# A streaming encoder step on one core: x's tail loaded first, the first chunk's factors and evictions moved, and one addition moved at the end

## The chip, the cores and the metric

The kernel runs on one core of one Trainium2 chip. The metric is the time on the device in microseconds, smaller being better. Before the change it is the median of three runs, 586.95 us, with 585.12 and 587.8 as the ends.

## The reference

One inference step of a one-layer encoder over 512 prompt frames, 64 frames of a running stream ("sample") and 16 meta tokens, model width 1024, all in fp32:

```python
h = rmsnorm(x, norm1_g) @ w_in            # 1024 -> 2304: rq, rk, rv, rg, sq, sk, sv
rq, rk = rope(rq), rope(rk) * 64 ** -0.5  # retention: 4 heads, 64 wide, values 128
sq, sk = rope(rmsnorm(sq)), rope(rmsnorm(sk))       # 8 query and 2 key heads of 64
o_r = rmsnorm(retention(rq, rk, rv, state)) * silu(rg)
o_s = window_attention(sq, sk, sv, meta_k, meta_v, sinks)    # window 128, chunks of 64
x = x + concat(o_r, o_s) @ w_out
x = x + moe(rmsnorm(x, norm2_g))          # best of 4 groups, best 2 of its 8 experts, SwiGLU, 256 wide
```

It also returns the retention states and the newest 128 rows of keys and values, for the prompt and for the sample.

## The kernel before

**Tiles.** The tokens lie in five tiles: tiles 0 to 3 hold 128 prompt frames each, tile 4 ("the tail", `TAIL`) the 64 sample frames and the 16 meta tokens. They are worked in the order tail, 0, 1, 2, 3 (`ORDER`). The input projection is cut into five chunks of columns: first SKV (keys and values of the attention, 256 wide), then SQ (its queries), RQK, RV and RG, each 512 wide; two halves of the output projection follow. Each chunk and tile is one job on TensorE in two halves of the contraction (four blocks of 128 each).

**Precision.** x and the weights are split into a high part (rounded by a cast) and a low part (the difference). For a weight entry, ScalarE casts (L1522, `hi`) and GpSimd subtracts (L859, `lo`). For x, TensorE transposes four blocks against the identity (L986), DVE multiplies by norm1's factors into `part` (L1718), ScalarE casts to `xT_hi` (L1464), and DVE subtracts to `xT_lo` (L1705). Every product is three matmuls (L1038), or two with both parts of the 64 sample rows side by side in the columns of one weight load (L1032). For that second form DVE copies the sample's low parts beside the high ones (L1756), which `xT_end` does at its end.

**Rows' factors.** The squares of x are summed by ScalarE (`xsq`, L1457). `rstd1` on DVE makes the reciprocal roots for all five tiles in twelve small steps (L1725 and the helper at L286 to L296). Evictions of the first chunk (ScalarE, L1478 and L1479) multiply by them; `sums` squares the keys (ScalarE L1497, DVE reduces), `root` takes their roots on DVE, `post` rotates keys (from L1804) with tables that `tables` makes (L1743: norm factor times cosine and sine, for keys and for queries), and the tail's own keys before that.

**The order.** `plan()` writes one list of steps from `before[s]`, job `s`, `after[s]` and `behind[s]`, where s counts the half jobs: 0 to 9 are SKV's, 10 on are SQ's. Every engine goes through the same list and issues what is its own, so the order of steps in that list is the order of the instructions in each engine's queue. In the list, `hi`/`lo` are weight entries 0 to 3 (SKV) and 4 to 11 (SQ), `xT` the transposes of a tile's half with what follows them. The accumulators of SKV's tail and tile 0 are the two that SQ's first jobs use again, so that SQ starts when these two are evicted. SQ's tile 1 waits for the tail's q, which DVE sums from two parts (L1987). `cache_in` and `meta_v` are ScalarE's issues of small transfers (the cache of keys, values and state; shifted copies of the values), and `meta_v` also one copy on DVE (L1849).

**Loading.** Transfers are issued by three queues. SyncE's begins with norm1's factors `g1T`, the identity, the sample's x and the meta tokens, then weights and x of tiles 1 and 3, then SQ's weights; ScalarE's begins with weights and x of tiles 0 and 2; GpSimd's loads five small tensors (`small_in`).

**The experts.** 32 experts go through in 16 pairs. SyncE streams their weights through 18 buffers of 1 MB, which lie partly where the attention's tensors were, so that the first loads wait for the retention's last rows and later ones for the pairs to free a buffer. Rows are gathered, passed through, and scattered by GpSimd.

**The end.** Each tile's two rows of expert output are read back. DVE adds the two for tiles 0 and 4 (`row_in`, L2234), GpSimd for tiles 2 and 3 (L963), TensorE for tile 1. DVE then adds the last pairs' part from the accumulators (`sums_in`, L2283), in the order of the tiles, and SyncE writes each tile out:

```python
for i in (2, 3):
    dve.wait_ge(rows_clear, 2 + i)    # GpSimd's addition of tile i is done
    sums_in(i)
row_in(4)
sums_in(4)
```

Of the kernel before, what the change touches and what calls it, by code (L numbers as in the profile page):

```python
# [7 lines left out]
ALU = mybir.AluOpType  # L8
# [82 lines left out]
def plan():  # L91
# [17 lines left out]
    before[0] += weights(0, 1) + turned(0) + weights(2, 3) + turned(1) + [("small_in",)]  # L109
    before[1] += [("xsq", ORDER[0])] + turned(2)  # L110
    before[2] += weights(4)
    before[3] += [("xsq", ORDER[1])] + turned(3) + weights(5)
    before[4] += [("xsq", ORDER[2])] + weights(6, 7)
    before[5] += weights(8) + turned(4) + [("xsq", ORDER[3]), ("xsq", ORDER[4]), ("xT_end",), ("rstd1",)] + weights(9)
    before[6] += weights(10) + [("evict", SKV, t) for t in ORDER[:3]] + [("sums", SKV, t) for t in ORDER[:3]]
    before[6] += weights(11) + [("tables",)]
# [16 lines left out]
    after[s + 1] += [("post", SKV, TAIL), ("post", SKV, 0)]  # L133
    after[s + 2].append(("cache_in",))
    after[s + 3].append(("meta_v",))
# [164 lines left out]
def stream_step(nc, consts, x_prompt, x_sample, cache_ret_state, cache_swa_k, cache_swa_v,  # L300
# [6 lines left out]
    NCONST = at["zeros"][0]  # L307

# [12 lines left out]
    with ExitStack() as ctx:  # L321
# [372 lines left out]
        def _(sp):  # L694
# [20 lines left out]
            n_id = at["ident"][1]  # L715
            sp.dma_start(g1T[:, :], norm1_g.rearrange("o (p k) -> p (o k)", k=KD)).then_inc(id_in, 16)
            sp.dma_start(cst[:, 0:n_id], consts[:, 0:n_id]).then_inc(id_in, 16)
# [6 lines left out]
            for k in range(KD):  # L724
                load_weights(sp, SQ, k)
                if k == 3:
                    sp.dma_start(cst[:, n_id:], consts[:, n_id:NCONST]).then_inc(c_in, 16)
# [239 lines left out]
        def _(pe):  # L967
# [22 lines left out]
            def job(c, t, half, b):  # L990
# [15 lines left out]
                if c == SKV:  # L1006
                    pe.wait_ge(xt_hi, 2 * i + half + 1)
                    pe.wait_ge(xt_lo, 2 * i + half + 1)
# [413 lines left out]
        def _(act):  # L1422
# [15 lines left out]
            xp = x_prompt.rearrange("o (t p) d -> p (o t) d", p=P)  # L1438
            for k in (0, 2):
# [242 lines left out]
        def _(dve):  # L1682
# [17 lines left out]

            def xT_low(n):
# [6 lines left out]
            def xT(t, half, b):  # L1708
# [5 lines left out]
                if n > 2:  # L1714
                    dve.wait_ge(xt_lo, n - 2)
# [14 lines left out]
            def tables(b):  # L1730
                dve.wait_ge(c_in, 16)
                dve.wait_ge(g_in, 16 * 5)
                step(ts(neg_sinks[:, :], sinks[:, :], -1.0, None, ALU.mult))

                dve.wait_ge(xt_ps, 2 * NT)
                h = HD // 2
                for a, table, by in ((1, rope_gk, 1.0), (0, rope_gq, HD ** -0.5)):
# [597 lines left out]
```

## Time and profile before

| what | value |
|---|---|
| median of three runs | 586.95 us |
| profiled execution | 586.21 us, its span 584.4 us |
| TensorE busy (PE) | 506.3 us, 87% of the span |
| DVE, ACT, POOL busy | 268.5, 130.4, 155.6 us |
| chain that ended last | PE 51%, SPq 16%, DVE 13%, DMA 11% |
| mean granted clock of TensorE | 0.939 |

PE is TensorE, ACT ScalarE, POOL GpSimd, SP SyncE; a q behind a name is an engine's issuing queue. The span is the profiled execution from its first to its last instruction; its own time is 1.8 us longer. A timeline row gives start and length in us, the engine, the line, the operation with what it writes and reads, how many, and in brackets the idle time of the engine just before it with what ended that.

### The profile page before, as it was taken

What the parts mean: (1) busy time and instruction counts of PE and PEld (TensorE: products, weight loads), DVE (VectorE), ACT (ScalarE), POOL (GpSimd) and SP (SyncE); (2) the same over time, 40 slices, a digit from 0 to 9 for tenths busy, and PEclk for the clock granted to TensorE, in tenths of its full rate; (3) what the DMA queues carried; (4) which work ended last, traced back from release to release, by engine and by line L of the source; (5) the groups of instructions that cost most, each with busy time, mean ns of one, the idle gap of its engine ahead of it and who ended that gap; (6) DMA issues with size and microseconds to landing.
All of it is one profiled execution on the core that took longest, in us unless ns stands there. A gap on an engine that the chain in (4) does not pass through costs nothing.

```text
span 584.4 us, 7830 instructions
## 1 busy us (share of the span) xinstructions
PE 506.3 (87%) x2898; PEld 321.1 (55%) x2898; DVE 268.5 (46%) x592; ACT 130.4 (22%) x351; POOL 155.6 (27%) x279
## 2 busy tenths in 40 slices
PE   3968898999999999889995399999988977687985
PEld 2956676776777677668784363333433333233333
DVE  2778778768453565562325613323332112122435
ACT  3743153444545422230211100000000000000110
POOL 3633664112304544640304110211122011100003
PEclk9978897999999999999997579999999889798998
DMA  8422030022025922209936998899999999999997
GB/s 284 152 73 52 21 126 1 2 73 73 2 70 172 314 90 83 77 18 343 420 131 247 371 375 337 325 414 417 421 420 420 418 419 420 422 420 422 410 405 248
DMA packets 35031, 144.75 MB, mean 248 GB/s; under 512 B 5842, under 2 KB 8994, under 8 KB 23216
## 3 DMA queue, kind: packets, MB, share of 16 engines
q1 hardware_dynamic: 26608, 130.01, 57.0%
q0 software_dynamic: 4528, 9.01, 4.1%
q10 hardware_dynamic: 3856, 5.21, 2.8%
q8 instruction: 24, 0.39, 0.3%
q14 instruction: 15, 0.12, 0.1%
HBM read 138.16 MB, written 17.30 MB: 266 GB/s over the span
## 4 chain that ended last, share of the span: by engine, by line
PE 51%; SPq 16%; DVE 13%; DMA 11%; issue 5%; ACT 4%; POOL 0%; ACTq 0%; DVEq 0%; POOLq 0%
PE banks L1038 20%; SPq L705 10%; PE banks L1262 9%; SPq L713 5%; DMA w_moe_b<-in_w_up_dram 5%; PE banks L1277 4%; PE banks L1096 2%; DMA w_moe_a<-y_d 2%; PE banks L1256 2%; PE banks L1342 2%; DMA y_d<-y_sb,idx 1%; PE banks L1215 1%; PE banks L1130 1%; PE banks L1032 1%; DMA w_raw<-in_w_in_dram 1%
## 5 line engine op out<-in xcount | busy, mean ns | idle before, releaser
L859 POOL TENSOR_TENSOR w_lo<-w_raw,w_hi 128x512 fp32r<-128x512 f32 x52 | 69.3, 1348 | 126.9 <-ACT w_hi L1522 125.3
L1262 PE MATMUL banks<-w_moe_b,xgT 128*64 128x512 f32 x224 | 71.6, 650 | 15.7 <-DMA w_moe_b<-in_w_up_dram 8.6
L1262 PE MATMUL banks<-w_moe_a,xgT 128*64 128x512 f32 x224 | 69.9, 633 | 5.5 <-DMA w_moe_a<-in_w_up_dram 5.5
L2168 DVE SCALAR_TENSOR_TENSOR glu<-banks,wr,glu 128x256 f32<-128x256 f32 x15 | 7.2, 483 | 113.0 <-ACT glu L1646 113.0
L1262 PEld LDWEIGHTS banks<-w_moe_b,xgT 128*64 128x64 f32 x224 | 22.8, 148 | 56.8 <-issue 54.3
L1646 ACT ACTIVATE glu<-banks,wr 128x256 f32<-128x256 f32 x15 | 7.1, 474 | 206.6 <-PE banks L1262 187.4
L1038 PE MATMUL banks<-w_hi,xT_hi_a 128*128 128x512 f32 (+3 forms) x124 | 50.8, 410 | 1.5 <-issue 1.4
L1038 PE MATMUL banks<-w_lo,xT_hi_a 128*128 128x512 f32 (+3 forms) x124 | 48.4, 390 | 0.0
L1038 PE MATMUL banks<-w_hi,xT_lo_a 128*128 128x512 f32 (+3 forms) x124 | 48.0, 387 | 0.0
L1038 PE MATMUL banks<-w_hi,xT_hi_b 128*128 128x512 f32 (+3 forms) x92 | 37.1, 403 | 0.1
L1262 PEld LDWEIGHTS banks<-w_moe_a,xgT 128*64 128x64 f32 x224 | 22.0, 145 | 26.5 <-issue 24.1
L1038 PE MATMUL banks<-w_lo,xT_hi_b 128*128 128x512 f32 (+3 forms) x92 | 35.1, 381 | 0.0
L1522 ACT CAST w_hi<-w_raw 128x512 fp32r<-128x512 f32 x52 | 31.0, 617 | 17.2 <-DMA w_raw<-in_w_out_dram 11.1
L1038 PE MATMUL banks<-w_hi,xT_lo_b 128*128 128x512 f32 (+3 forms) x92 | 34.7, 377 | 0.0
L1566 ACT ACTIVATE probs<-banks,soft,rstd_qk 128x208 f32<-128x208 f32 (+1 forms) x40 | 20.6, 519 | 57.8 <-DVE soft L1879 57.8
L1277 PE MATMUL banks<-w_moe_a,actT 128*64 128x512 f32 x144 | 32.6, 592 | 0.0
L1038 PEld LDWEIGHTS banks<-w_hi,xT_hi_a 128*128 128x128 f32 (+1 forms) x124 | 24.0, 194 | 7.3 <-issue 1.9
L2132 DVE TENSOR_TENSOR xgT<-banks,g_both 128x1024 f32<-128x1024 f32 x16 | 19.5, 1219 | 18.4 <-PE banks L1256 18.4
L1038 PEld LDWEIGHTS banks<-w_hi,xT_lo_a 128*128 128x128 f32 (+1 forms) x124 | 24.0, 193 | 5.1
L1038 PEld LDWEIGHTS banks<-w_lo,xT_hi_a 128*128 128x128 f32 (+1 forms) x124 | 24.1, 194 | 3.8
L1277 PEld LDWEIGHTS banks<-w_moe_a,actT 128*64 128x64 f32 x144 | 11.5, 137 | 19.4 <-issue 19.4
L908 POOL DMA_INDIRECT y_sb<-hn_d,idx x6 | 6.0, 1008 | 57.4 <-DMA y_d<-y_sb,idx 27.4
(329 smaller groups left out, 940.7 us busy)
## 6 DMA issues: line engine op xcount, KB each, us to landing
w_moe_a<-in_w_down_dram SPq DMA_DIRECT2D x20, 1024.0 KB, 27.6
w_moe_a<-in_w_gate_dram SPq DMA_DIRECT2D x16, 1024.0 KB, 11.4
w_moe_a<-in_w_up_dram SPq DMA_DIRECT2D x16, 1024.0 KB, 13.4
w_moe_b<-in_w_gate_dram SPq DMA_DIRECT2D x14, 1024.0 KB, 23.9
w_moe_b<-in_w_up_dram SPq DMA_DIRECT2D x14, 1024.0 KB, 26.3
w_moe_b<-in_w_down_dram SPq DMA_DIRECT2D x10, 1024.0 KB, 27.9
w_raw<-in_w_in_dram SPq DMA_DIRECT2D x34, 256.0 KB, 4.0
y_d<-in_consts_dram SPq DMA_DIRECT2D x9, 512.0 KB, 10.0
```

The costliest lines, as they stand in the source:

```text
L705: sp.dma_start(units(gu_at(p, e, m), 1)[:, 0, :], v[2 * p + e]).then_inc(gu_in[p % 4], 16)
L713: sp.dma_start(dn_at(p, e), down_v[2 * p + e]).then_inc(dn_in[p % 4], 16)
L859: nc.gpsimd.tensor_tensor(w_lo[:, s, :], w_raw[:, s, :], w_hi[:, s, :].bitcast(F32), ALU.subtract).then_inc(split, 1)
L1038: l = mm(into[0:R, 0:width], a, w, start=(kk == 0 and q == 0), stop=(kk == KD - 1 and q == 2))
L1096: l = mm(sideA[64 * c2:64 * c2 + 64, b, 256 * hl + dst:256 * hl + dst + n], sqT[gs, ORDER.index(t) % DEEP, 2 * hh + hl, CH * c2:CH * c2 + CH],
L1256: l = nc.tensor.transpose(into[:, k // 4, (k % 4) * P:(k % 4) * P + P], gv[:, k, :], ident)
L1262: l = mm(acc[64 * e:64 * e + 64, u, :].rearrange("p (m f) -> p m f", m=2), xgT[:, xu, k, 64 * e:64 * e + 64], units(at_e[e], 2)[:, :, k * ...
L1277: l = mm(acc[64 * e:64 * e + 64, 2 + n, :], actT[:, j, 64 * e:64 * e + 64], mats[e][:, j * D + n * 512:j * D + n * 512 + 512], start=(j == ...
L1342: l = mm(acc[64 * e:64 * e + 64, 0, m * FF:m * FF + FF], xgT[:, 0, k, 64 * e:64 * e + 64], units(gu_at(0, e, m), 1)[:, 0, k * FF:k * FF + ...
L1522: nc.scalar.copy(w_hi[:, s, :], w_raw[:, s, :]).then_inc(hi_done, 1)
L1566: af(probs[0:R, q, hl, :], sideA[0:R, b, 256 * hl:256 * hl + KEYS], ACT.Exp, scale=rstd_qk[0:R, h + hl:h + hl + 1], bias=soft[0:R, q, 2 + ...
L2132: tt(xgT[:, u], at[:, 0:2, :].rearrange("p b (j n) -> p (b j) n", j=4), g2T.unsqueeze(2).to_broadcast([P, KD, P]), ALU.mult).then_inc(xg_e ...
```

## The change

At the start, ScalarE's queue issues the identity and `g1T` ahead of its weights, and SyncE's starts with the sample's x and the meta tokens. `small_in` moves to the front of GpSimd's steps. The squares of each tile's x move ahead by some steps; the weight entries 7 to 11 move behind the rows' factors. The sample's copies of the low parts become a step of their own, `tail_low`, ahead of tile 3's transposes rather than behind its low parts, with the counts in TensorE's and DVE's waits adapted. The first three tiles' evictions, formerly in one group, go tile by tile with their squares, with weight entries between. `tables` is divided: the keys' table stays in the first chunk, the queries' table goes behind the keys' rotation, and `cache_in` and `meta_v` come to that place too, one and two half jobs earlier. At the end tile 4's two rows are added ahead of the wait for GpSimd's addition of tile 3.

```diff
-    before[0] += weights(0, 1) + turned(0) + weights(2, 3) + turned(1) + [("small_in",)]
-    before[1] += [("xsq", ORDER[0])] + turned(2)
-    before[2] += weights(4)
-    before[3] += [("xsq", ORDER[1])] + turned(3) + weights(5)
-    before[4] += [("xsq", ORDER[2])] + weights(6, 7)
-    before[5] += weights(8) + turned(4) + [("xsq", ORDER[3]), ("xsq", ORDER[4]), ("xT_end",), ("rstd1",)] + weights(9)
-    before[6] += weights(10) + [("evict", SKV, t) for t in ORDER[:3]] + [("sums", SKV, t) for t in ORDER[:3]]
-    before[6] += weights(11) + [("tables",)]
+    before[0] += [("small_in",)] + weights(0, 1) + turned(0) + [("xsq", ORDER[0])] + weights(2, 3) + turned(1)
+    before[1] += [("xsq", ORDER[1])] + turned(2)
+    before[2] += weights(4) + [("xsq", ORDER[2])]
+    before[3] += turned(3) + [("tail_low",)] + weights(5)
+    before[4] += [("xsq", ORDER[3])] + weights(6)
+    before[5] += turned(4) + [("xsq", ORDER[4]), ("xT_end",), ("rstd1",)] + weights(7, 8)
+    before[6] += [(kind, SKV, t) for t in ORDER[:2] for kind in ("evict", "sums")] + weights(9) + [("tables", 1)]
+    before[7] += [(kind, SKV, ORDER[2]) for kind in ("evict", "sums")] + weights(10)
+    before[8] += weights(11)
...
-    after[s + 1] += [("post", SKV, TAIL), ("post", SKV, 0)]
-    after[s + 2].append(("cache_in",))
-    after[s + 3].append(("meta_v",))
+    after[s + 1] += [("post", SKV, TAIL), ("post", SKV, 0), ("tables", 0), ("cache_in",), ("meta_v",)]
...
-            sp.dma_start(g1T[:, :], norm1_g.rearrange("o (p k) -> p (o k)", k=KD)).then_inc(id_in, 16)
-            sp.dma_start(cst[:, 0:n_id], consts[:, 0:n_id]).then_inc(id_in, 16)
...
-                    pe.wait_ge(xt_lo, 2 * i + half + 1)
+                    pe.wait_ge(xt_lo, 2 * i + half + (1 if i < 3 or (i == 3 and half == 0) else 3))
...
+            act.dma_start(cst[:, 0:N_ID], consts[:, 0:N_ID]).then_inc(id_in, 16)
+            act.dma_start(g1T[:, :], norm1_g.rearrange("o (p k) -> p (o k)", k=KD)).then_inc(id_in, 16)
             for k in (0, 2):
                 load_weights(act, SKV, k)
...
+            def tail_low(b):
                 for half in range(2):
-                    dve.wait_ge(xt_lo, 2 * NT)
+                    dve.wait_ge(xt_lo, half + 1)
                     nc.vector.tensor_copy(xT_hi[half][:, :, P * TAIL:P * TAIL + DEC],
...
             for i in (2, 3):
+                if i == 3:
+                    row_in(4)
                 dve.wait_ge(rows_clear, 2 + i)
                 sums_in(i)
-            row_in(4)
             sums_in(4)
```

## Rows read from the trace of the kernel before

**Rows 1.** Busy time by stretch: us, each engine's busy us, PEclk, DMA share, GB/s.
```profile
63.00:66.00 3.00, 3.00 (x9) 2.33 (x8) 2.90 (x6) 0.00 (x0) 2.25 (x8) 0.56 0.00 0
...
285.00:560.00 275.00, 233.19 (x1132) 112.43 (x1133) 82.57 (x160) 15.16 (x32) 36.50 (x45) 0.91 0.94 380
```

**Rows 2.** Timeline of TensorE, 0 to 62 us.
```profile
8.72 3.01 PE L986 MATMUL banks<-cst,x_sb 80*128 80x80 f32 x16 [8.72 <-DMA x_sb<-in_meta_tokens_dram]
13.13 0.47 PE L1038 MATMUL banks<-w_hi,xT_hi_a 128*80 128x256 f32 x1 [1.39 <-issue]
...
24.16 1.06 PE L986 MATMUL banks<-cst,x_sb 128*128 128x128 f32 x8
...
37.21 0.80 PE L1032 MATMUL banks<-w_hi,xT_hi_a 128*128 128x512 f32 x1 [4.49 <-ACT sv L1479]
...
51.81 0.69 PE L1038 MATMUL banks<-w_hi,xT_hi_a 128*128 128x512 f32 x1
...
61.95 0.87 PE L1061 MATMUL banks<-cst,sq 128*128 128x128 f32 x4 [1.94 <-DVE sq L1843]
```

**Rows 3.** Timeline of DVE, 20 to 62 us.
```profile
23.07 0.68 DVE L1705 TENSOR_TENSOR xT_lo_a<-rv,xT_hi_a 128x512 fp32r<-128x512 f32 x1
...
27.49 1.73 DVE L1705 TENSOR_TENSOR xT_lo_a<-rv,xT_hi_a 128x512 fp32r<-128x512 f32 x1 [0.46 <-ACT xT_hi_a L1464]
...
30.95 1.34 DVE L1756 CAST xT_hi_a<-xT_lo_a 128x256 fp32r<-128x256 f32 x1
...
33.50 0.16 DVE L1725 TENSOR_SCALAR ms<-ssq 128x5 f32<-128x5 f32 x1
...
35.70 0.17 DVE L296 TENSOR_TENSOR rstd<-root 128x5 f32<-128x5 f32 x1
...
40.49 1.21 DVE L1743 SCALAR_TENSOR_TENSOR rope_gq<-cst,qk_g 128x320 f32<-128x320 f32 x3
42.22 0.69 DVE L1779 TENSOR_REDUCE ssq_qk<-squares 128x8 f32<-128x512 f32 x1 [0.51 <-DVE rope_gq L1743]
...
51.02 0.73 DVE L1987 SCALAR_TENSOR_TENSOR sq<-banks,rstd,squares 64x512 f32<-64x512 f32 x1
...
55.46 0.68 DVE L1849 COPY v_own<-sv 16x1024 f32<-16x1024 f32 x1
...
59.01 2.80 DVE L1843 TENSOR_TENSOR sq<-h_a,h_b 128x256 f32<-128x256 f32 x2
```

**Rows 4.** Chain of waits to 130 us: start, length, what it went through.
```profile
2.89 7.80 DMA w_raw<-in_w_in_dram
...
62.83 4.11 PE banks L1038 x12
...
67.94 2.98 PE banks L1038 x12
```

**Rows 5.** Transfers issued before 20 us: size, median us from issue to landing.
```profile
x_sb<-in_x_sample_dram SPq DMA_DIRECT2D x1, 256.0 KB, 5.7
cst<-in_consts_dram SPq DMA_DIRECT2D x1, 64.0 KB, 3.1
```

**Rows 6.** Timeline of ScalarE, 36 to 62 us.
```profile
38.14 0.62 ACT L1522 CAST w_hi<-w_raw 128x512 fp32r<-128x512 f32 x1
...
54.38 0.69 ACT L1490 ACTIVATE sq<-banks,rstd 128x512 f32<-128x512 f32 x1 [1.46 <-issue]
```

**Rows 7.** Timeline of all engines, 569 to 585 us.
```profile
575.07 2.41 POOL L963 TENSOR_TENSOR w_moe_a<-w_moe_a 128x1024 f32<-128x1024 f32 x1 [1.86 <-DMA w_moe_a<-y_d]
...
577.51 1.22 DVE L2283 TENSOR_TENSOR w_moe_a<-w_moe_a,banks 128x1024 f32<-128x1024 f32 x1 [1.84 <-POOL w_moe_a L963]
578.65 1.21 DVE L2234 TENSOR_TENSOR w_moe_b<-w_moe_b 64x1024 f32<-64x1024 f32 x1
```

**Rows 8.** Timelines of DVE and GpSimd, 108 to 111 us.
```profile
108.80 1.57 POOL L859 TENSOR_TENSOR w_lo<-w_raw,w_hi 128x512 fp32r<-128x512 f32 x1 [2.80 <-ACT w_hi L1522]
109.26 1.66 DVE L1826 TENSOR_TENSOR rqk<-h_a,cst 128x512 f32<-128x512 f32 x1
```

More of the change, by code:

```diff
@@ L307, in stream_step @@
     NCONST = at["zeros"][0]
+    N_ID = at["ident"][1]
     hn_d = nc.dram_tensor("hn_d", [T_TOK, D], F32, kind="Internal").ap()
@@ L726, in _ @@
                 if k == 3:
-                    sp.dma_start(cst[:, n_id:], consts[:, n_id:NCONST]).then_inc(c_in, 16)
+                    sp.dma_start(cst[:, N_ID:], consts[:, N_ID:NCONST]).then_inc(c_in, 16)
             for c in (RQK, RV, RG):
@@ L1699, in _, with lows_done @@
             dve.sem_inc(ssq_clear, 1)
+            def lows_done(n):
+                return n if n < 8 else n + 2
             def xT_low(n):
@@ L1714, in xT @@
                 if n > 2:
-                    dve.wait_ge(xt_lo, n - 2)
+                    dve.wait_ge(xt_lo, lows_done(n - 2))
                     dve.wait_ge(xt_hi, n - 2)
@@ L1728, in rows_factor, with tables @@
                 nc.vector.tensor_copy(r1_up, rstd1[0:DEC, TAIL:TAIL + 1]).then_inc(rstd_ready, 1)
[L1730 to L1735, printed above, removed]
-                h = HD // 2
-                for a, table, by in ((1, rope_gk, 1.0), (0, rope_gq, HD ** -0.5)):
-                    g = qk_g[:, a:a + 1, :].to_broadcast([P, NT, HD])
-                    g_hi = qk_g[:, a:a + 1, h:].to_broadcast([P, NT, h])
-                    g_lo = qk_g[:, a:a + 1, 0:h].to_broadcast([P, NT, h])
-                    for out, x, y in ((table[:, 0], cos_t, g), (table[:, 1, :, 0:h], sin_t[:, :, 0:h], g_hi),
-                                      (table[:, 1, :, h:], sin_t[:, :, h:], g_lo)):
-                        step(stt(out=out, in0=x, scalar=by, in1=y, op0=ALU.mult, op1=ALU.mult))
+            def tables(a, b):
+                h = HD // 2
+                if a:
+                    dve.wait_ge(c_in, 16)
+                    dve.wait_ge(g_in, 16 * 5)
+                    step(ts(neg_sinks[:, :], sinks[:, :], -1.0, None, ALU.mult))
+                else:
+                    dve.wait_ge(xt_ps, 2 * NT)
+                    dve.wait_ge(sq_done, NT)
+                table, by = (rope_gk, 1.0) if a else (rope_gq, HD ** -0.5)
+                g = qk_g[:, a:a + 1, :].to_broadcast([P, NT, HD])
+                g_hi = qk_g[:, a:a + 1, h:].to_broadcast([P, NT, h])
+                g_lo = qk_g[:, a:a + 1, 0:h].to_broadcast([P, NT, h])
+                for out, x, y in ((table[:, 0], cos_t, g), (table[:, 1, :, 0:h], sin_t[:, :, 0:h], g_hi),
+                                  (table[:, 1, :, h:], sin_t[:, :, h:], g_lo)):
+                    step(stt(out=out, in0=x, scalar=by, in1=y, op0=ALU.mult, op1=ALU.mult))
             def counts(b):
@@ L2021, in logit @@
                     tt(logits[0:R, t, :], logits[0:R, t, :], ps, ALU.add).then_inc(lg_ev, 1)
-            does = {"xT": xT, "xT_end": xT_end, "rstd1": rows_factor, "tables": tables, "counts": counts, "root": key_factors, "evict": evict, "sums": sums, "post": post,
+            does = {"xT": xT, "xT_end": xT_end, "tail_low": tail_low, "rstd1": rows_factor, "tables": tables, "counts": counts, "root": key_factors, "evict": evict, "sums": sums, "post": post,
                     "gate": gate_of, "gate2": gate_sum, "meta_v": meta_v, "qT": qT, "score": score, "norm": norm,
```

1 line of the change is left out of this document (removed).

## The prediction

> **What bounds the kernel now.** I read the page's chain of waits first: its largest shares are TensorE and the issuing of transfers on SyncE's queue. The table of stages divides these in time [rows 1]: from 285 to 560 us the DMA engines are 0.94 busy, the expert weights stream at 380 GB/s, and nothing that the change touches lies there. But this stream can only start once the retention is done (SyncE waits for the last mixed rows), its later loads wait for buffers that the pairs of experts free, and those pairs start behind the router. So every microsecond won before some 255 us, in a stage where TensorE sets the pace, moves the whole stream forward with it; nothing in the kernel is tied to a fixed time. The timeline of TensorE then shows where the first 62 us have holes [rows 2]: it starts at 8.72 (x's tail landed last), its first projection starts at 13.13, it sits idle for 4.49 us ahead of 37.21 (evictions of the first chunk), its third tile of the second chunk, q of tile 1, starts only at 51.81, and 1.94 us are idle ahead of 61.95. The reader is to see in DVE's timeline [rows 3] that the releasers of 37.21 and 51.81 are one chain: tile 3's low parts (two alike from 27.49, until 30.9), the tail's copies (two alike from 30.95, until 33.5), the rows' factors until 35.87, keys' sums at 42.22, rotation of keys, and the sum of the tail's q at 51.02. I call 35.87 E, the time at which the rows' factors are ready. 51.81 is E + 15.9.
>
> **The start.** ScalarE now issues the identity and norm1's factors, so on SyncE's queue the tail's x moves up by two issues, 0.91 us (from 1.66 to 0.75), and so do the weights and x behind it; on ScalarE's queue the weights and x of tiles 0 and 2 move back by two issues, 0.9 us. Ahead of the first projection stand: the second pair of weights (issued 2.89, landed 7.80 later, [rows 4]), its cast of 0.6 and GpSimd's subtraction of 1.3 to 1.6. That transfer is now issued at about 1.95. If it takes 7.80 as before, the first projection comes 0.9 earlier. If it is as quick as the identity was (3.1, [rows 5]), it would land at 5.1, and tile 0's x, on the other queue, and its transposes would be last, about 4 us earlier than now. I take the sample's x as the nearest row (5.7, [rows 5]): landed 7.65, first projection at 10.3, **2.8 us earlier**. GpSimd's five small loads, some 3 us of issuing, now stand ahead of its first subtraction, but that one waits for a cast until about 5, so they are hidden; if the subtraction were held by 1 us, the projection would be too.
>
> **To E.** Tile 3's transposes started at 24.16, 11.0 behind the first projection, with TensorE dense between; so now at 21.3. From there to the last low part DVE took 6.8 us: two parts, three low parts, of which the last two took 1.73 each against 0.68 for the same shape at 23.07 [rows 3], since GpSimd subtracted three weights beside them and ScalarE cast these weights ahead of tile 3. The change casts only one weight there (entry 6) and leaves 7 and 8 for later: five steps of 0.65 and 0.5 for the first four transposes make 4.0. **2.8 less.** The tail's two copies (1.3 each, [rows 3]) leave this place: **2.6 less**. They come back ahead of tile 3, where DVE sat idle for over 1 us waiting for transposes; they cost 0.7 unhindered, 2.7 otherwise, and the cover is these idle times; if it is gone, E is up to 1.5 later. Squares of x go to ScalarE earlier: seven casts of weights and eight of x at 0.55 and four squares at 1.25 fill some 13 us between 5 and 21, which just fits. The factors' twelve small steps take 2.4 (33.50 to 35.87, [rows 3]). But entries 7 and 8 are now subtracted on GpSimd just beside them, and steps with two inputs in SBUF wait then: from 0 to two subtractions of 1.3, 2.6. I take 1.9, near the upper end, **1.9 more**. E: 35.87 - 2.8 - 2.8 - 2.6 + 1.9 = 29.6, **6.3 earlier**.
>
> **From E to the second chunk.** Two tiles' evictions free the accumulators 1.34 behind E, as now (37.21), 1.4 with the squares between: TensorE goes on at about 31, with at most 1.3 us idle in place of 4.49. That isn't the gain itself: it waits again for the keys and for 51.81. Keys' sums need all five tiles: on ScalarE five evictions with squares at 0.7 (three took from E to 38.14, [rows 6]) and three casts at 0.55 make E + 5.2; now they start at E + 6.35. Behind them: 0.7 sum, 2.5 root, 4.6 both rotations, then the moved tables of q (1.21 and 0.1, [rows 3]) and meta's values (0.95, at 55.46 before), and 0.75 for the tail's q: E + 16.0. One subtraction (the entry cast just ahead) falls beside the keys' rotation and holds it 1.1 as one held the root before. So the second chunk's tile 1 starts at E + 17.2, **1.3 later** against E than now. Bounds: 0.2 (no hold) and 2.5 (two).
>
> **From there to 67 us.** ScalarE's four issues of meta's copies no longer stand ahead of q's eviction of tile 0, which began 2.63 behind the tail's q only because of them (idle 1.46 ahead of 54.38, [rows 6]); meta's copy on DVE is gone from there too. The sum of tile 0's q comes 1.1 earlier against the tail's q, and its last step, which two subtractions held for 2.06 (2.80 for two steps of 0.38 at best each, [rows 3]), is done before GpSimd has finished its own root. So the 1.94 idle ahead of 61.95 goes, **1.9 less**, and with it the slow job behind it, 4.11 against 2.98 for the same twelve matmuls [rows 4], with the granted clock at 0.56 from 63 to 66 [rows 1], most of it at 1.2 GHz: **1.1 less**. Late next is TensorE itself. In exchange its idle time ahead of tile 1 grows from 2.3 to some 4 us, and the first matmuls behind it stay at half rate a little longer: **0.4 more**.
>
> **The end.** Tile 4's rows (1.21, [rows 7]) now stand ahead of the sum of tile 3, in the 1.84 us in which DVE waited for GpSimd. If they fitted, the last transfer would go 1.2 earlier. But GpSimd adds tile 3's rows from 575.07 to 577.48, and DVE is free only at 575.67. In [rows 8] DVE's 512 columns from two SBUF inputs, started at 109.26 while GpSimd worked until 110.37, ended at 110.92, 0.55 behind it, and took 1.66. The same here: rows of tile 4 end at about 578.6, both sums follow, 581.05 in place of 581.1, and tile 3's output, 512 KB, leaves 1.2 later, just ahead of the last one, which can cost up to 0.6. I take 0; the ends are -1.2 and +0.6. The Trainium skill says the same of the cause (SBUF — State Buffer, the part on its two physically separate sides): the port pair shared by the two is an exclusive lock, held for the whole instruction, and the other engine fully blocks. By that rule this part of the change is worth nothing; by the idle time alone it is worth 1.2.
>
> **Sum.** -6.3 + 1.3 - 1.9 - 1.1 + 0.4 + 0 = -7.6. The profiled execution took 586.21 (span 584.4), 0.7 under the median of 586.95; I set the difference against the median: 579.4.
>
> **The rivals.**
> - The first transfers don't come earlier (both queues share the same DMA engines, which are full from 3 us on): only 0.9 of the 2.8 is won, the rest stays: -5.7, 581.3. For it: the total of bytes is unchanged. Against: the tail waited behind ScalarE's transfers, which now start later. 0.13.
> - DVE is the bound from 60 to 100 us: what is won at 61.95 comes back as a wait for scores, and the larger hole ahead of tile 1 costs 1.5 in clock: -6.3 + 2.5 = -3.8, 583.1. For it: a hole of 1.9 us there is left in DVE's favour only if its order holds. Against: DVE's own chain starts as much earlier. 0.13.
> - More than I count: no subtraction meets the factors (-1.9) and the end gains (-1.2): -10.7, 576.3. 0.10.
> - The gain isn't carried to the end: the weight stream ends last and is bound by bytes [rows 1]; if its start didn't follow the retention, only the end's part would count: 586.5. 0.04.
> - Slower: TensorE now starts at about 5, then has holes while it waits for tile 0's x and weights. Its granted clock could then rise late. From 8.72 sixteen transposes took 3.01, 0.19 each; at 24.16 eight larger ones took 1.06, 0.13 each [rows 2]: it was at the slower rate first. Behind the rise the first chunk has some 15 us of work. A job that takes 2.98 quick took 4.11 when the slow rate covered about half of it; if all 15 us went at that rate throughout, it would be some 13 more: 592.3. From a rise that comes 15 us later than counted it is slower than before. Against: it had a hole of 1.4 us ahead of 13.13 too [rows 2] and the rate rose all the same. 0.04.
> The forecast itself has 0.56, with 577.3 to 581.5 as its own range.
>
> **How the numbers follow.** The time is that of the forecast, 579.4. The range for 8 in 10 reaches up to the second rival and down to near the third: 576.0 to 583.6. About 0.5% (2.9 us) is what a measurement of this kernel can tell from no change. Forecast and the first three rivals lie beyond it, less the part of the second that falls short: faster 0.89; within 0.5%: 0.07, the fourth and that part; slower 0.04.
>
> **What would show it.** Right: first transposes near 5, the first projection near 10.3, the factors' last step near 29.6, tile 1 of the second chunk at 46 to 47, no idle time ahead of tile 0's q, and the same distance from there to the end as now; at the end the rows of tile 4 stretched to 2 us or more beside GpSimd's addition. Wrong: weights still landing near 10, the factors' steps with more than two waits, a hole of over 2 us between 60 and 100 that wasn't there, or low clock after 15 us.

## The result and the profile after

The changed kernel takes 583.2 us (median of 8, 580.85 to 587.92) against 586.81 us for the one before (median of 8, 585.12 to 588.37): a ratio of 0.9941, 95% interval 0.9917 to 0.9964, so 3.5 us faster with an interval of 2.1 to 4.9. The forecast was 579.4 us, 7.5 us faster. The direction was right, the size a little under half of what was forecast.

The profiled execution of the changed kernel took 580.85 us, its fastest of eight, with a span of 579.0 against 584.4 before. So this pair of profiles differs by 5.4 us, the medians by 3.6. Both numbers have to be explained, and they are two questions.

The page of the changed kernel, busy time of each engine with its share of the span:
```profile
PE 504.2 (87%) x2898; PEld 319.8 (55%) x2898; DVE 262.4 (45%) x592; ACT 130.4 (23%) x351; POOL 155.3 (27%) x279
```
DVE is busy 6 us less (268.5 before). A step that stands waiting for GpSimd counts as busy, and in the first 62 us, where fewer do, DVE has 38.8 us in place of 42.0; where the other half went isn't shown.

TensorE's timeline of the changed kernel, 0 to 62 us, against [rows 2] (L983 is L986 of before, L1036 is L1038, L1030 is L1032, L1059 is L1061):
```profile
5.18 1.30 PE L983 MATMUL banks<-cst,x_sb 80*128 80x80 f32 x8 [5.18 <-DMA x_sb<-in_meta_tokens_dram]
11.09 1.97 PE L983 MATMUL banks<-cst,x_sb 128*128 128x128 f32 x8 [4.61 <-DMA x_sb<-in_x_prompt_dram]
12.71 0.56 PE L1036 MATMUL banks<-w_hi,xT_hi_a 128*80 128x256 f32 x1
13.07 0.41 PE L1036 MATMUL banks<-w_lo,xT_hi_a 128*80 128x256 f32 x1
13.29 0.41 PE L1036 MATMUL banks<-w_hi,xT_lo_a 128*80 128x256 f32 x1
...
16.89 0.28 PE L1036 MATMUL banks<-w_lo,xT_hi_b 128*80 128x256 f32 x1
17.01 0.28 PE L1036 MATMUL banks<-w_hi,xT_lo_b 128*80 128x256 f32 x1
...
34.26 0.80 PE L1030 MATMUL banks<-w_hi,xT_hi_a 128*128 128x512 f32 x1 [2.81 <-ACT sv L1479]
...
50.51 0.79 PE L1036 MATMUL banks<-w_hi,xT_hi_a 128*128 128x512 f32 x1 [2.33 <-DVE sq L1996]
...
58.55 0.60 PE L1059 MATMUL banks<-cst,sq 128*128 128x128 f32 x4
```
The tail's transposes start at 5.18 as forecast, but the first projection starts at 12.71 in place of 10.3: tile 0's x lands late, and TensorE is idle for 4.61 us in front of it. The later holes are smaller than before (2.81 for 4.49), and the one ahead of tile 0's q is gone (58.55 has no bracket, where [rows 2] had 1.94). E, the end of the factors' last step, is 32.59 in the next view.

DVE's timeline of the changed kernel, 22 to 57 us, against [rows 3]:
```profile
22.98 0.29 DVE L1765 CAST xT_hi_a<-xT_lo_a 128x256 fp32r<-128x256 f32 x1
...
27.18 0.68 DVE L1708 TENSOR_TENSOR xT_lo_b<-rv,xT_hi_b 128x512 fp32r<-128x512 f32 x1
28.07 0.17 DVE L1728 TENSOR_SCALAR ms<-ssq 128x5 f32<-128x5 f32 x1 [0.22 <-ACT rqk L1457]
...
28.68 1.26 DVE L287 TENSOR_TENSOR root<-root,ms 128x5 f32<-128x5 f32 x1
29.97 1.22 DVE L288 TENSOR_SCALAR root<-root 128x5 f32<-128x5 f32 x1
...
32.42 0.17 DVE L295 TENSOR_TENSOR rstd<-root 128x5 f32<-128x5 f32 x1
...
38.80 0.69 DVE L1788 TENSOR_REDUCE ssq_qk<-squares 128x8 f32<-128x512 f32 x1 [3.47 <-ACT squares L1497]
...
44.76 1.40 DVE L1815 TENSOR_TENSOR h_b<-sk,rope_gk 128x256 f32<-128x256 f32 x1
...
49.71 0.74 DVE L1996 SCALAR_TENSOR_TENSOR sq<-banks,rstd,squares 64x512 f32<-64x512 f32 x1
...
56.27 0.76 DVE L1852 TENSOR_TENSOR sq<-h_a,h_b 128x256 f32<-128x256 f32 x2
```
Two of the factors' small steps took over 1.2 us where their neighbours take 0.17, and one step of the keys' rotation took 1.40 where the like one at 44.31 took 0.42. GpSimd's timeline of the same kernel shows what they met, two subtractions and then one:
```profile
28.63 2.54 POOL L856 TENSOR_TENSOR w_lo<-w_raw,w_hi 128x512 fp32r<-128x512 f32 x2 [1.93 <-ACT w_hi L1522]
...
44.39 1.49 POOL L856 TENSOR_TENSOR w_lo<-w_raw,w_hi 128x512 fp32r<-128x512 f32 x1 [5.23 <-ACT w_hi L1522]
```

The chain of waits of the changed kernel around 62 us, against [rows 4]:
```profile
59.15 2.78 PE banks L1036 x12
61.94 1.00 PE banks L1094 x12
```
The job that took 4.11 us in [rows 4] takes 2.78. The windows of the changed kernel, against [rows 1]:
```profile
63.00:66.00 3.00, 3.00 (x15) 2.43 (x16) 1.55 (x8) 1.21 (x5) 2.40 (x7) 1.00 0.01 3
```
The granted clock is 1.00 in place of 0.56.

The first expert load of SyncE's queue, changed kernel and then the kernel before:
```profile
258.15 0.33 SPq L705 DMA_DIRECT2D w_moe_a<-in_w_gate_dram  x1
```
```profile
263.21 0.33 SPq L705 DMA_DIRECT2D w_moe_a<-in_w_gate_dram  x1
```
The first scores (61.94) come 5.0 us earlier than before (62.83 + 4.11 = 66.94, [rows 4]), the stream 5.06 earlier, the span ended 5.4 earlier. In this pair whatever is won by 62 us is carried through to the end, as the prediction had it.

The end of the changed kernel, GpSimd and DVE, against [rows 7]:
```profile
569.84 2.41 POOL L960 TENSOR_TENSOR w_moe_a<-w_moe_a 128x1024 f32<-128x1024 f32 x1 [1.71 <-DMA w_moe_a<-y_d]
571.16 2.17 DVE L2243 TENSOR_TENSOR w_moe_b<-w_moe_b 64x1024 f32<-64x1024 f32 x1 [0.52 <-DMA w_moe_b<-y_d]
```
Tile 4's rows moved into the wait for GpSimd and took 2.17 us there, ending at 573.33, 1.08 behind GpSimd's 572.25.

### The profile page after: what moved, and what is told of

The parts are those of the page before. It is cut to its first block, busy times and chain, and to the rows that moved or that the text cites. A ratio compares the mean times of both kernels' runs of the same rounds, so it can differ in the third digit from the quotient of the medians.

```text
span 579.0 us, 7830 instructions
## 1 busy us (share of the span) xinstructions
PE 504.2 (87%) x2898; PEld 319.8 (55%) x2898; DVE 262.4 (45%) x592; ACT 130.4 (23%) x351; POOL 155.3 (27%) x279
## 4 chain that ended last, share of the span: by engine, by line
PE 49%; SPq 16%; DVE 11%; DMA 10%; issue 4%; ACT 3%; POOL 1%; DVEq 0%; POOLq 0%; ACTq 0%
PE banks L1036 19%; SPq L705 10%; PE banks L1260 9%; DMA w_moe_b<-in_w_up_dram 5%; SPq L713 5%; PE banks L1275 4%; PE banks L1094 2%; DMA w_moe_b<-y_d 2%; PE banks L1254 2%; PE banks L1340 2%; DMA y_d<-y_sb,idx 2%; PE banks L1128 1%; PE banks L1179 1%; PE banks L1174 1%; PE banks L1213 1%
## 5 line engine op out<-in xcount | busy, mean ns | idle before, releaser
L1036 PE MATMUL banks<-w_hi,xT_hi_a 128*128 128x512 f32 (+3 forms) x124 | 50.2, 405 | 2.3 <-DVE sq L1996 2.3
L1036 PE MATMUL banks<-w_lo,xT_hi_a 128*128 128x512 f32 (+3 forms) x124 | 47.9, 386 | 0.0
L1036 PE MATMUL banks<-w_hi,xT_lo_a 128*128 128x512 f32 (+3 forms) x124 | 47.6, 384 | 0.0
L1036 PE MATMUL banks<-w_hi,xT_hi_b 128*128 128x512 f32 (+3 forms) x92 | 36.8, 400 | 0.0
L1036 PE MATMUL banks<-w_lo,xT_hi_b 128*128 128x512 f32 (+3 forms) x92 | 35.0, 381 | 0.0
L1036 PE MATMUL banks<-w_hi,xT_lo_b 128*128 128x512 f32 (+3 forms) x92 | 34.9, 379 | 0.0
L1036 PEld LDWEIGHTS banks<-w_hi,xT_hi_a 128*128 128x128 f32 (+1 forms) x124 | 23.7, 191 | 7.4 <-DVE sq L1996 2.5
L1036 PEld LDWEIGHTS banks<-w_hi,xT_lo_a 128*128 128x128 f32 (+1 forms) x124 | 23.7, 191 | 5.0
L1036 PEld LDWEIGHTS banks<-w_lo,xT_hi_a 128*128 128x128 f32 (+1 forms) x124 | 23.7, 191 | 3.7
```

Source lines behind the costliest of these rows:

```text
L1036: l = mm(into[0:R, 0:width], a, w, start=(kk == 0 and q == 0), stop=(kk == KD - 1 and q == 2))
```

## Experiments

Ratios are against the kernel before, timed beside each variant; in microseconds they are taken of 586.4. In brackets stands the 95% interval. The theory at the outset was that the small loads, now issued first, delay the large ones in the DMA engines. The rival was that two queues that share the engines bring tile 0's x no sooner, whatever the small loads do.

**The five small loads back in their old place.**
```diff
-    before[0] += [("small_in",)] + weights(0, 1) + turned(0) + [("xsq", ORDER[0])] + weights(2, 3) + turned(1)
+    before[0] += weights(0, 1) + turned(0) + [("xsq", ORDER[0])] + weights(2, 3) + turned(1) + [("small_in",)]
```


> The changed kernel with GpSimd's five small loads put back behind weight entry 3 and tile 0's transposes; all else as changed. Theory of the small loads: these broadcasts sit in the DMA engines at 6 to 10 us (share 1.03 at only 287 GB/s from 6 to 9 us) and slow the transfer of tile 0's x and of weight entry 2 on ScalarE's queue. Then tile 0's transposes start near 8.5 to 9 instead of 11.09, entry 2's cast near 10.5 instead of 13.0, the factors are ready (E) near 30 instead of 32.6, and the kernel is 2 to 2.5 us faster than the changed one (0.990 against the kernel before). Theory of the queues: ScalarE's transfers are late because two more stand ahead of them and SyncE's large x transfers take the engines; then tile 0's transposes still start at 10.5 to 11.1 and the time stays at 0.994.

Measured: 581.1 us, ratio 0.9909 (0.9889 to 0.993), 5.3 us faster than before where the change alone is 3.5. TensorE's timeline of this kernel:
```profile
8.31 1.97 PE L983 MATMUL banks<-cst,x_sb 128*128 128x128 f32 x8 [1.75 <-DMA x_sb<-in_x_prompt_dram]
11.14 0.47 PE L1036 MATMUL banks<-w_hi,xT_hi_a 128*80 128x256 f32 x1 [0.86 <-issue]
```
Tile 0's transposes start 2.8 us sooner than with the loads first (11.09), the first projection 1.6 sooner. The DMA view of the first 20 us shows the cause (queue: packets, MB, share of the 16 engines; then a transfer with its KB and the us from issue to landing; "x2" is the median of tile 0's and tile 2's x), first of the changed kernel, then of this one:
```profile
q0 software_dynamic: 160, 0.08, 9.2%
...
x_sb<-in_x_prompt_dram ACTq DMA_DIRECT2D x2, 512.0 KB, 10.6
...
sinks<-in_attn_sinks_dram POOLq DMA_DIRECT2D x1, 4.0 KB, 8.0
```
```profile
q0 software_dynamic: 148, 0.07, 1.7%
...
x_sb<-in_x_prompt_dram ACTq DMA_DIRECT2D x2, 512.0 KB, 7.7
...
sinks<-in_attn_sinks_dram POOLq DMA_DIRECT2D x1, 4.0 KB, 4.5
```
Tile 0's x alone was issued at 2.15 in both and landed 8.9 us later in the changed kernel, 6.1 us later here. 9.2% of 20 us is 1.84 us of every engine, for 0.08 MB; issued later, about the same packets took 0.34. The windows of both (us, busy time of PE, PEld, DVE, ACT and POOL, granted clock, DMA share, GB/s), changed kernel first:
```profile
6.00:9.00 3.00, 0.48 (x4) 0.24 (x2) 1.56 (x3) 2.78 (x6) 2.52 (x2) 1.00 1.03 287
9.00:12.00 3.00, 0.91 (x4) 0.91 (x5) 0.00 (x0) 0.00 (x0) 0.21 (x1) 1.00 0.97 271
```
```profile
6.00:9.00 3.00, 1.25 (x8) 1.02 (x7) 0.98 (x2) 0.65 (x2) 1.26 (x1) 1.00 1.02 391
9.00:12.00 3.00, 2.14 (x10) 1.77 (x10) 2.17 (x3) 2.62 (x6) 1.57 (x2) 1.00 1.06 395
```
The engines are full in both, but move 279 GB/s over these 6 us with the small loads among them and 393 without. (393 - 279) x 6 us is 0.68 MB, more than the 512 KB of tile 0's x. A DMA share of 1.0 doesn't say that the bandwidth is used. The rival's part is true as well: with the loads late, tile 0's x still took 6.1 us, where it took 4.9 in the kernel before and was issued 0.9 sooner. But it doesn't decide.

**Identity and g1T back on SyncE's queue**, ahead of the tail's x; all else as changed.
```diff
-            act.dma_start(cst[:, 0:N_ID], consts[:, 0:N_ID]).then_inc(id_in, 16)
-            act.dma_start(g1T[:, :], norm1_g.rearrange("o (p k) -> p (o k)", k=KD)).then_inc(id_in, 16)
...
+            sp.dma_start(g1T[:, :], norm1_g.rearrange("o (p k) -> p (o k)", k=KD)).then_inc(id_in, 16)
+            sp.dma_start(cst[:, 0:N_ID], consts[:, 0:N_ID]).then_inc(id_in, 16)
             load_x(TAIL)
```


> The changed kernel with the identity and norm1's factors back on SyncE's queue ahead of the sample's x; small loads still first. Theory of the small loads: tile 0's x still suffers, so the first projection is at 13 or later (both handicaps), E near 33.5, 0.995 to 0.996 against before. Theory of the queues: ScalarE's transfers are as early as in the kernel before, tile 0's x is there by 8.8, the first projection at about 13.1 because entry 1 lands near 10.7, E near 32.5, time as the changed kernel, 0.994.

Measured: 585.38 us, 0.9977 (0.9958 to 0.9997). This is slower than either theory said. The first projection starts at 14.88, later than in the kernel before (13.13). The small loads come first here too, and from 6 to 12 us the engines move 224 and 235 GB/s. The new queues are worth about 2.1 us beside early small loads.

**The end in its old order** (`row_in(4)` behind the loop again).
```diff
             for i in (2, 3):
-                if i == 3:
-                    row_in(4)
                 dve.wait_ge(rows_clear, 2 + i)
                 sums_in(i)
+            row_in(4)
```


> The changed kernel with tile 4's rows behind the sum of tile 3 again, as before the change. Theory of the shared port (DVE's addition of two SBUF inputs is held while GpSimd adds): the end's part of the change is worth 0, so this is the same as the changed kernel, 0.994, and the distance from the end of GpSimd's second addition to the last transfer's issue stays 3.5 us. Rival: the order was worth up to 1.2 us, so this is 0.996.

Measured: 583.26 us, 0.9942 (0.9925 to 0.996), against 0.9941 with the new order. This part is worth nothing that can be measured, as forecast.

**The tail's q ahead of the tables and of meta's values on DVE.**
```diff
-    after[s + 1] += [("post", SKV, TAIL), ("post", SKV, 0), ("tables", 0), ("cache_in",), ("meta_v",)]
+    after[s + 1] += [("post", SKV, TAIL), ("post", SKV, 0), ("cache_in",), ("meta_v",)]
+    after[s + 2].append(("tables", 0))
+    after[s + 3].append(("meta_dve",))    # meta_v's copy on DVE alone
```


> The changed kernel with the queries' table and DVE's copy of the meta values behind the sum of the tail's q instead of ahead of it (ScalarE's part stays where the change put it). Theory that DVE's chain sets the start of tile 1's q job: that job starts 2.0 to 2.2 us earlier (48.4 instead of 50.5, idle 2.33 ahead of it gone), and the first score near 60.5 instead of 61.9: 1 to 1.5 us faster than the changed kernel, 0.992. Rival: the table is needed for the rotation of q anyway, so the first score stays at 61.9 and the time at 0.994.

Measured: 582.7 us, 0.9935 (0.9916 to 0.9954). The sum of the tail's q starts at 48.39 although this execution's first projection was 0.84 later, so 2.2 sooner against it. The time differs by 0.4, which the intervals can't tell from nothing.

**Both of these edits together** (loads late, q first).


> The changed kernel with both mends: the small loads late and the queries' table and DVE's meta copy behind the tail's q. If the two gains are independent (2.1 us and 0.4 us by the runs so far), 580.7, 0.990. Theory that DVE's order only fills another hole: 0.991, as with the small loads alone.

Measured: 580.78 us, 0.9916 (0.9888 to 0.9945), the same as the late loads alone. The sum of the tail's q starts at 45.37 and the first scores at 58.84, 3.1 us earlier than in the changed kernel, yet the stream starts at 258.14, the same as there (258.15). In this execution the lead went to the clock: TensorE's granted clock was 0.91 from 180 to 200 us and 0.89 from 240 to 256, where the changed kernel has 1.00 in both, and that is an estimated 3.5 us (the missing 0.09 of 20 us and 0.11 of 16). In the last kernel of this section, with the same order behind 60 us and 1.00 in both stretches, a first score at 59.68 led to a stream at 255.93. Why the median doesn't show the lead either stays open.

**The changed plan alone**: queues, small loads and end as before.


> The kernel before with the changed plan of the first two chunks alone: start queues, small loads and end as before. Theory that the plan itself carries most (low parts free of GpSimd, tail's copies out of the way, ScalarE's issues early): first projection at 13.1 as before, factors ready 2 us earlier than before (near 34), first score near 64: 0.994 to 0.995. Rival, that the start carries most and the plan's gain is taken back by the factors held beside entries 7 and 8: 0.997 to 0.999.

Measured: 583.45 us, 0.9957 (0.993 to 0.9984), between what the two theories said. Against the queues in their old place with early small loads (0.9977) it differs by the place of these loads and by the end, which is worth nothing.

**The new queues alone**: the kernel before, with identity and g1T on ScalarE's queue.


> The kernel before with the new order of the start's queues alone (identity and norm1's factors on ScalarE's queue, tail first on SyncE's); small loads, plan and end as before. First projection near 11.1, 2 us earlier; with additive parts 0.996 to 0.997. Rival: the gain is lost by 37 us because DVE's low parts set the pace there: 0.999.

Measured: 583.73 us, 0.9945 (0.9924 to 0.9967). The first projection starts at 11.26 and not at 13.13. Queues alone are worth 3.2 us (1.9 to 4.5), the plan alone 2.5 (0.9 to 4.1); their sum, 5.7, is near what both give with late small loads (5.3), and the change itself gives 3.5. So within these intervals the parts add up, and what is missing is the small loads. Three pairs of kernels differ only by the place of these loads, one of them by the end too: 0.9941 against 0.9909, 0.9977 against 0.9957, and 0.9935 against 0.9916. That is 1.9, 1.2 and 1.1 us for the early loads; no pair is clear of its intervals alone, but all three point the same way.

**The factors free of GpSimd's subtractions** (entries 7 and 8 behind the first two evictions; small loads late).
```diff
-... ("xT_end",), ("rstd1",)] + weights(7, 8)
-    before[6] += [(kind, SKV, t) for t in ORDER[:2] for kind in ("evict", "sums")] + weights(9) + [("tables", 1)]
+... ("xT_end",), ("rstd1",)]
+    before[6] += [(kind, SKV, t) for t in ORDER[:2] for kind in ("evict", "sums")] + weights(7, 8, 9) + [("tables", 1)]
```


> The changed kernel, small loads late, and weight entries 7 and 8 cast and subtracted behind the first two evictions, so that GpSimd does not work beside the rows' factors. Theory of the shared port: the twelve factor steps take 2.4 us again in place of 4.5, the factors are ready near 29; ScalarE's casts then come later, keys' sums start at the factors + 6.3 in place of + 5.2: 1 us net, 0.989. Rival: GpSimd's subtractions now hold the keys' root instead and the first score stays: 0.991.

Measured: 581.82 us, 0.9918 (0.9893 to 0.9942), no faster than the late loads alone (0.9909). The factors' last step moved from 31.17 to 29.20, as it should, but the tail's q is summed at 48.26 in place of 48.59: 2.0 us of lead shrank to 0.3 behind the factors. DVE's timeline in this kernel shows where:
```profile
36.62 0.69 DVE L1788 TENSOR_REDUCE ssq_qk<-squares 128x8 f32<-128x512 f32 x1 [4.50 <-ACT squares L1497]
37.34 0.89 DVE L1802 TENSOR_SCALAR ms<-ssq_qk 128x10 f32<-128x10 f32 x1
```
The idle time ahead of the keys' sums grew from 3.46 to 4.50, since ScalarE now casts three entries behind the first two evictions. And the first step of the keys' root takes 0.89 in place of 0.17, beside GpSimd's subtractions, which run until 38.20: the rival was right in part.

**Both kernels again**, for the spread between executions of one code.


> The kernel before, unchanged, against itself: what a comparison tells where there is nothing to tell. Ratio 1.000 within 0.002. Its profile also shows how much the distance from the first score to the first load of expert weights differs from run to run (196.3 us in the profile before, 196.3 to 201.5 in those since).

> The changed kernel, unchanged. Theory that the profiled 580.85 was a lucky execution and 3.5 us is the gain: ratio 0.994 again, first projection at 12.5 to 13, factors ready at 32 to 33, and a profile whose distance from the first score to the first expert load is longer than 196.3 in most executions. Rival: the gain is 5.4 as in the pair of profiles, ratio 0.991.

Measured: before 586.15 us, 0.9981 (0.996 to 1.0001) against itself, changed 582.88 us, 0.9937 (0.9915 to 0.996). So a ratio can be off by about 0.2%, 1.1 us, without any cause in the code. The chain of waits of the kernel before in this second execution, against [rows 4]:
```profile
58.14 2.80 DVE sq L1843 x2
...
61.71 2.78 PE banks L1038 x12
64.48 1.00 PE banks L1096 x12
```
The wait that held tile 0's q is there again (the two steps on DVE take 2.80), but the job behind it takes 2.78 and not 4.11: the slow job was not the code's. Nor is all of E. In the first execution tile 0's first transposes (15.75) took 1.91, in the second (15.72) 1.10, and E is 35.87 and 35.07.

**A third execution of each.**


> The kernel before once more, for a third profile: first score at 64.4 or 66.9 as in the two so far, by whether the job behind the hole at 60 us runs at the slower rate; distance from the first score to the first expert load 196 to 201.5.

> The changed kernel once more, for a third profile: first score at 61.9 to 63.0, distance to the first expert load 196 to 201.5. Over three profiles each, the changed kernel's first score should be 3 to 3.5 us earlier, as the medians say, and not the 5.0 of the first pair.

Measured: 584.5 and 581.94 us (one execution each). The chain of the kernel before agrees with its second execution:
```profile
61.80 2.78 PE banks L1038 x12
64.58 1.00 PE banks L1096 x12
```
The first scores of the kernel before start at 66.9, 64.5 and 64.6, of the changed one at 61.9, 63.0 and 62.3: means of 65.3 and 62.4, 2.9 us apart. From there to the first expert load it takes 196.3, 197.2 and 197.3 us before, and 196.2, 197.3 and 197.4 in the changed kernel: the same.

**Which of the small loads.** Three spread one row over 128 partitions (the norms of q and k, 32 KB each as written, and the sinks, 4 KB); two are plain (8 and 2 KB). First the sinks alone in the old place, the others early:


> The changed kernel with only the load of the sinks (4 KB, spread from 8 values to 128 partitions) moved back behind weight entry 3; the other four small loads stay first. Theory that this one load clogs the DMA engines: software queue's share up to 20 us falls from 9.2% to under 4%, 6 to 9 us moves near 390 GB/s in place of 287, tile 0's transposes near 8.5, time 0.991 as with all five late. Rival, that each of the five costs its part: share 5 to 8%, transposes at 10 to 10.8, 0.993 to 0.994.

Measured: 582.57 us, 0.9925 (0.9897 to 0.9953), which can't be told from 0.9937 for the changed kernel beside it. Tile 0's transposes start at 11.26, no sooner than in the changed kernel (11.09), though the throughput from 9 to 12 us is back at 391 GB/s.

Then the norms of q and k late, and all three late (one execution each):


> The changed kernel with only the two loads of the norm factors of q and k (64 values spread to 128 partitions, 32 KB each) moved back; the sinks' and the two plain ones stay first. If the two are the clog: tile 0's transposes near 8.5 to 9.5 in place of 11.1 to 11.9, 6 to 9 us near 390 GB/s. If the sinks' load is a clog of its own: transposes still above 10 and 9 to 12 us under 300 GB/s. One look, the time says nothing at this size.

> The changed kernel with the three loads that spread one row to 128 partitions moved back; the two plain ones (8 KB and 2 KB) stay first. If spreading is what clogs: tile 0's transposes at 8.3 to 9.7 and 6 to 9 us near 390 GB/s, as with all five late. If any early load on GpSimd's queue does it: above 10.

Measured: 580.38 and 581.09 us (one execution each, too few to rank). Tile 0's transposes start at 10.69 and 10.07; with all five late and these queues they start at 8.31, 8.97, 9.04 and 9.63 in four kernels, with all five early at 11.06 to 11.93 in five profiles. With the norms late the engines still move 263 GB/s from 6 to 9 us. With the three late:
```profile
6.00:9.00 3.00, 0.68 (x6) 0.44 (x4) 0.98 (x2) 0.69 (x2) 1.26 (x1) 1.00 0.97 376
```
So most of the throughput comes back with the three spreading ones, and no single load explains the delay. Whether the two plain loads, 10 KB together, cost anything (10.07 against 9.63 at most) can't be told from one execution.

**The findings put together**: small loads late, q first, the factors free, and entry 1's weights as the first transfer of SyncE's queue.
```diff
+            load_weights(sp, SKV, 1)
             load_x(TAIL)
...
             for k in (1, 3):
-                load_weights(sp, SKV, k)
+                if k == 3:
+                    load_weights(sp, SKV, k)
                 load_x(k)
```


> All mends together: small loads late, queries' table and meta copy behind the tail's q, entries 7 and 8 behind the first two evictions, and weight entry 1 first on SyncE's queue ahead of the sample's x. If the three plan mends add up (the small loads alone gave 5.2 us against before): first projection near 10.3, factors ready near 28.5, tail's q near 45, first score near 58, 0.988 to 0.989. Rival: ScalarE's later casts and the second chunk's holes take it back, 0.991.

Measured: 579.74 us, 0.9885 (0.9849 to 0.9921); the changed kernel has 0.9937 beside it. It is the fastest of all by its median, 3.1 us under the changed kernel; the two intervals just touch. TensorE's timeline (L987 and L1034 are L983 and L1030 of the changed kernel):
```profile
9.51 1.97 PE L987 MATMUL banks<-cst,x_sb 128*128 128x128 f32 x8 [0.18 <-DMA x_sb<-in_x_prompt_dram]
11.45 0.47 PE L1040 MATMUL banks<-w_hi,xT_hi_a 128*80 128x256 f32 x1
...
31.19 0.50 PE L1034 MATMUL banks<-w_hi,xT_hi_a 128*128 128x512 f32 x1 [1.62 <-ACT sv L1483]
...
38.41 0.80 PE L1034 MATMUL banks<-w_hi,xT_hi_b 128*128 128x512 f32 x1 [0.52 <-POOL w_lo L860]
```
The hole ahead of the second chunk is down to 1.62, and the next waits are for the low parts of the weights on GpSimd (five of 0.4 to 0.6 us): that is what the entries moved behind the factors bring. Entry 1 as the first transfer brought nothing that shows: the first projection starts at 11.45 and not near 10.3, against 11.14, 10.66 and 11.30 in the other kernels with these queues, this plan and late loads. The factors are ready at 29.52 and the first scores start at 59.68, each 1 to 2 us later than expected.

## Why the prediction was wrong in size

**The start: this step failed.** The prediction counted 2.8 us for an earlier first projection; the trace has 0.4 (13.13 to 12.71), and over three profiles each it is 0.1 (means of 13.02 and 12.91). The sentence that broke is that GpSimd's five small loads "are hidden". It weighed their issuing against the first subtraction, and that part holds. It left out that their packets go through the same 16 DMA engines as x and the weights, in the very stretch where these set the pace. With late loads the first projection comes 1.6 us sooner in the first pair, 1.8 over all profiles with these queues (mean of 11.09 in four kernels), and 1 to 2 us of the time come back. The remaining 0.9 of the 2.8 is missing even then. The weights, for which the prediction took 5.7 us from [rows 5], were not the last thing behind the changed start: there it is tile 0's x, which landed 8.9 us after its issue, 6.1 with late loads, and 4.9 in the kernel before. Of this the prediction had nothing in its sum; it named tile 0's x only for the case of quick weights. (Its own rows also give 3.0 and not 2.8 for weights that land at 7.65 in place of 10.69.) The Trainium skill (DMA: Bandwidth & Descriptors, the part on queues, rings and completion order) says that a DMA engine takes turns between the queues that have work, packet by packet. The runs fit with that in so far as 0.08 MB of small packets hold up far larger transfers, but they don't show the turns; why a packet of this queue costs 0.18 us of an engine early (1.84 x 16 / 160) and 0.04 later (0.34 x 16 / 148) they don't show either.

**To E.** Forecast 29.6, measured 32.59, which is 3.3 earlier than before and not 6.3. From the first projection to E it took 19.9 against 22.7 before, 2.9 less where the prediction had 3.5 (2.8 + 2.6 - 1.9): right within 0.6. (The five steps and the 0.5 of the prediction add to 3.75, not 4.0; measured from tile 3's transposes to the last low part: 4.55.) The tail's copies took 0.29 each, unhindered; tile 3's last low parts took 0.98, 1.00 and 0.68; the two blocked steps of the root cost 2.1 where 1.9 was taken. Over three profiles each, E is 35.4 before (35.87, 35.07, 35.15) and 32.5 after (32.59, 33.08, 31.97): the profile that the prediction read had the latest E of the three.

**From E to tile 1 of the second chunk.** Forecast 1.3 later (its terms add to E + 17.1, it says 17.2), measured 2.0 (17.9 against 15.9). The step of the keys' rotation was held once, by one subtraction, as counted. The rest, 0.7, is ScalarE: the keys' sums were to start at E + 5.2 and start at E + 6.2 (38.80), since an eviction with its squares takes 0.85 of it (33.61 to 34.45), not 0.7; the steps behind took 0.3 less than summed.

**From there to 67 us.** The wait ahead of tile 0's q went, 1.9 as forecast: DVE's last step took 0.76 for the pair in place of 2.80. The 1.1 for the slow job was a term that should not have stood in the sum as the change's gain. It is in one of three executions of the kernel before and depends on the granted clock of that execution. Had the prediction set it at 0, it would have said 580.5. (That job takes 2.78 in the other executions; the 2.98 of the prediction is another job.)

**The end.** Forecast 0, measured 0 (0.9942 against 0.9941). In [rows 8] DVE was free 0.55 behind GpSimd; here it was 1.08 behind, 2.17 us for an addition that took 1.21 alone [rows 7]. The rule of the Trainium skill that the prediction set against the idle time (SBUF — State Buffer, the part on its two physically separate sides: the shared port pair is an exclusive lock) gave the right answer, and this trace agrees with it.

**Sum and medians.** Of the profile pair: -0.4 at the start, -2.9 to E, +2.0 to tile 1, -3.7 from there to the scores (1.9 the wait, 1.3 the slow job, the rest the denser work between), together -5.0, then 0.4 in the rest: 5.4 us of span. Forecast by the same steps: -2.8, -3.5, +1.3, -2.6. In this pair the start alone is 2.4 of the 2.6 us between -7.6 and -5.0; the other three differences (+0.6, +0.7, -1.1) nearly cancel. But that is luck of the pair, since the slow job of one execution is in the last of them. The means of three profiles each are the fairer account:

| step | forecast | one pair | three profiles each |
|---|---|---|---|
| first projection | -2.8 | -0.4 | -0.1 |
| from there to E | -3.5 | -2.9 | -2.7 |
| E to tile 1 of the second chunk | +1.3 | +2.0 | +2.1 |
| from there to the first scores | -2.6 | -3.7 | -2.2 |
| sum | -7.6 | -5.0 | -2.9 |

All four steps gave less than forecast: 2.7 of the 4.7 us that are missing lie in the start, 0.8 in each of the next two, 0.4 in the last. The medians say 3.5, and 2.9 lies inside their interval.

Of the rivals the first was nearest in its place (the transfers don't come earlier), but its reason was incomplete. The second has the nearest number, 583.1 against 583.2, and that is chance: its mechanism, DVE taking the lead back behind 62 us, would lengthen the way from the first scores to the first expert load, and that stayed the same (196.3 to 197.3 before, 196.2 to 197.4 after). The late rise of the clock didn't come. The granted clock can't show this, it reads 1.00 from 6 to 18 us in both; the matmuls do. Those of the first projection, 256 columns each, follow one another every 0.21 us in both kernels, which is 1.2 GHz, and later every 0.12 us: from 16.9 us in the changed kernel, from 17.9 in the one before. Two prices of the rivals are off: 15 us of work at half rate cost 15 more and not 13, and the fourth's own terms leave 586.95 and not 586.5. Nothing hangs on either.

## What to carry to other kernels

Count a transfer that moves ahead by its packets in the DMA engines, not only by its issue: here 78 KB from another queue cost a load of 512 KB 2.8 us where loading set the pace. Put into a forecast only those waits of the profile that the code causes; a job at half clock in one execution is to be seen in a second one first, and so is every time that the sum starts from. And a step freed on one engine is worth what the next wait leaves of it: find that wait before counting the gain.

## What was not expected of the hardware

Full DMA engines (share 1.02 and 1.03) moved 391 GB/s in one kernel and 287 in the other, and the only edit between them is the place of five loads of 78 KB in all. Which property of these packets does it stays open. Nor are they the only cause: the kernel before, whose small loads are issued much later, has such a stretch too, but a shorter one:
```profile
6.00:9.00 3.00, 0.28 (x2) 0.31 (x3) 0.00 (x0) 0.00 (x0) 0.29 (x1) 1.00 1.06 280
9.00:12.00 3.00, 2.73 (x16) 2.33 (x14) 1.26 (x3) 1.28 (x4) 0.59 (x1) 1.00 1.06 388
```
With late small loads and the new queues the slow stretch is from 3 to 6 us alone (279 GB/s), with early ones it lasts from 3 to 12 (270, 287, 271). What the early loads do is lengthen it.

The granted clock differs in stretches between executions of nearly the same code. The windows of the kernel with late small loads in its profiled execution (585.83 us, the slowest of its six; median 581.1), then of the changed kernel:
```profile
105.00:110.00 5.00, 3.19 (x21) 2.42 (x22) 3.80 (x11) 0.77 (x3) 0.30 (x1) 0.66 0.01 3
110.00:115.00 5.00, 5.00 (x25) 3.71 (x25) 4.24 (x12) 2.92 (x12) 0.00 (x0) 0.65 0.00 0
```
```profile
105.00:110.00 5.00, 5.00 (x45) 3.87 (x44) 3.80 (x11) 0.76 (x3) 0.31 (x1) 1.00 0.02 3
110.00:115.00 5.00, 5.00 (x45) 3.84 (x44) 4.24 (x12) 3.61 (x15) 0.00 (x0) 1.00 0.01 2
```
DVE does the same work in both, TensorE runs partly at 1.2 GHz in one. From the first scores to the first expert load, where all these kernels do the same work, the eighteen profiles took 196.2 to 201.5 us, so two single profiles can differ by 5 us with no edit to that stretch; what the medians say can't be read from one pair.
